# RWKV chunk part: 16 chunks at a time, odd chunks crossing to the other head's partitions, transition matrices per chunk, gate pieces inside the state chain

## What is computed

```python
def step(s, inp):
    r_t, w_t, k_t, v_t, a_t, b_t = inp
    sa = jnp.einsum('nhvk,nhk->nhv', s, a_t)
    s = (s * w_t[:, :, None, :] + sa[..., None] * b_t[:, :, None, :]
         + v_t[..., None] * k_t[:, :, None, :])
    return s, jnp.einsum('nhvk,nhk->nhv', s, r_t)
```

## Time and profile before

| | us |
|---|---|
| median of 3 runs | 2684.76 (2681.96 to 2686.89) |
| profiled execution | 2676.91 |
| its span, first to last instruction | 2675.2 |
| TensorE busy in it | 2428.9 |

### The profile page before, as it was taken

How to read it: one execution, slowest core, us unless ns; L and a number is a source line. 1 busy time by engine, 2 the same in 40 slices (tenths; PEclk the granted TensorE clock), 3 DMA queues, 4 the chain that set the end, 5 groups by cost and what they waited for, 6 DMA issues and landing times.

```text
span 2675.2 us, 39291 instructions
## 1 busy us (share of the span) xinstructions
PE 2428.9 (91%) x17425; PEld 1629.9 (61%) x17425; DVE 925.3 (35%) x1626; ACT 457.0 (17%) x946; POOL 158.9 (6%) x269
## 2 busy tenths in 40 slices
PE   5998999898888898888879997999999999999994
PEld 3665665557656766756756664666666666666563
DVE  3962441035325415415514333333331013333222
ACT  4114121122113113113130001111110001111002
POOL 2700000000000000000100000000000000000001
PEclk8999999999998998998979998999999999999997
DMA  6101233410020020011033311111101011110101
GB/s 220 60 20 41 78 120 111 132 56 16 11 58 15 8 61 15 8 38 46 3 137 106 128 32 32 32 33 33 33 29 44 24 64 33 33 33 25 36 20 65
DMA packets 111367, 139.72 MB, mean 52 GB/s; under 512 B 14818, under 2 KB 85975, under 8 KB 111184
## 3 DMA queue, kind: packets, MB, share of 16 engines
q1 hardware_dynamic: 96512, 115.38, 13.3%
q10 hardware_dynamic: 10992, 15.21, 1.6%
q0 software_dynamic: 3696, 6.64, 0.9%
HBM read 117.59 MB, written 19.61 MB: 51 GB/s over the span
## 4 chain that ended last, share of the span: by engine, by line
PE 79%; DVE 11%; ACT 4%; DMA 3%; issue 2%; DVEq 0%; ACTq 0%; SPq 0%; POOL 0%; POOLq 0%
PE ps L623 77%; DVE arena L1669 5%; DVE arena L1672 2%; DMA W<-in_w_in_dram 2%; PE ps L627 1%; DMA arena<-in_x_prompt_dram 1%; ACT Y L1437 1%; DVE arena L2100 1%; ACT arena L1316 0%; DMA Y<-in_x_prompt_dram 0%; DVE hT L1672 0%; DVE hT L1669 0%; DVE arena L2037 0%; ACT arena L1362 0%; DVE s5v L1669 0%
## 5 line engine op out<-in xcount | busy, mean ns | idle before, releaser
L623 PE MATMUL ps<-hT,W 128*128 128x352 f32 x4368 | 1337.1, 467 | 53.7 <-DMA W<-in_w_in_dram 17.8
L623 PEld LDWEIGHTS ps<-hT,W 128*128 128x128 f32 x4368 | 837.0, 193 | 528.8 <-issue 58.3
L623 PE MATMUL ps<-arena,W 128*128 128x352 f32 x1440 | 432.0, 463 | 14.7 <-DVE arena L1669 11.9
L623 PE MATMUL ps<-arena 64*64 64x64 f32 (+6 forms) x8744 | 354.6, 232 | 55.2 <-DVE arena L1669 22.0
L623 PEld LDWEIGHTS ps<-arena,W 128*128 128x128 f32 x1440 | 276.1, 192 | 170.1 <-DVE arena L1669 12.5
L623 PEld LDWEIGHTS ps<-arena 64*64 64x64 f32 (+3 forms) x8744 | 300.7, 137 | 115.7 <-issue 43.0
L1316 ACT ACTIVATE arena<-ps 128x512 f32<-128x512 f32 (+7 forms) x235 | 113.2, 489 | 523.1 <-PE ps L623 318.9
L2214 DVE TENSOR_SCALAR Y<-Y,PAR 128x1024 f32<-128x1024 f32 x88 | 49.0, 557 | 426.4 <-ACT Y L1316 424.7
L1316 ACT ACTIVATE Y<-ps 128x352 f32<-128x352 f32 (+3 forms) x220 | 69.9, 350 | 715.2 <-PE ps L623 536.5
L1669 DVE TENSOR_TENSOR arena<-arena 128x1056 f32<-128x1056 f32 (+6 forms) x181 | 166.8, 922 | 59.8 <-PE ps L623 44.9
L1669 DVE TENSOR_TENSOR arena<-ps,arena 128x256 f32<-128x256 f32 (+3 forms) x188 | 99.0, 527 | 220.4 <-PE ps L623 164.0
(11 more groups left out here) (250 smaller groups left out, 995.7 us busy)
## 6 DMA issues: line engine op xcount, KB each, us to landing
W<-in_w_ada_dram SPq DMA_DIRECT2D x12, 2048.0 KB, 9.4
W<-in_w_up_dram SPq DMA_DIRECT2D x22, 1024.0 KB, 6.5
gates<-arena ACTq DMA_DIRECT2D x72, 176.0 KB, 1.8
arena<-gates SPq DMA_DIRECT2D x24, 528.0 KB, 3.5
...
```

What stands on the lines that cost most here:

```text
L623: return nc.tensor.matmul(out, lhsT, rhs, start=start, stop=stop, skip_group_check=True)
```

## The change

The 16 chunks of a pair are taken together. In most products odd chunks cross: one side of the product (source or target) is the head's own half `hp`, the other is `sd` = `side(c, hh)`, and even and odd chunks write different banks. Two groups stay on the own half: `zt`, and the turned A. The halves of a level are now the first and the last 8 chunks. X starts as copies of the unit matrix (ACT) into which DVE copies the product of A and B by a mask, and XT is X turned by TensorE. LT has its own place for all 16 chunks.

The chain changes its form. Before it, and for all chunks, TensorE makes U0 (the part of U that doesn't depend on the state), a transition matrix `Gm` per chunk (unit matrix added by DVE), the state's change without the old state (accumulated in banks 4 and 5 and left open), a corrected R, and the output without the old state (left open in banks 0 and 1). A chain step is then one product of `Gm` with the state on top of the open bank and one scaling by DVE (`carry`), which writes the next state `Sb`; the product of the state with the corrected R finishes the output. After each of the 15 steps one product of gate group 5 or 6 is issued. The sample group's steps have gate group 7 in pieces of 2 products and the first half of group 8 between them; the final prompt state is turned at the end of the pair. The diff, with indentation and many lines left out:

```diff
-Vt, Bt, Kt_ = (carve(16164 + 512 * i, 8, RCH) for i in range(3))
-LA = carve(17700, 8, 2, RCH)
-KA = carve(18724, 8, 2, RCH)
-X, XT, Yb, LTm = (carve(19748 + 512 * i, 8, RCH) for i in range(4))
+LA, KA = carve(11940, 16, 2, RCH), carve(13988, 16, 2, RCH)
+X, XT = carve(16164, 16, RCH), carve(17188, 16, RCH)
+VB, Kt_ = carve(18212, 2, 2, 2, 4, RCH), carve(20260, 16, RCH)
+Yb, LT = carve(1065, 16, RCH), carve(3195, 16, RCH)
+LTm, Gm, Sb = carve(7332, 16, RCH), carve(8868, 16, RCH), carve(10404, 16, RCH)
+W0, U0, YT = X, Yb, LT
+dX, dXT, dLT, dYb, dLTm = (carve(8420 + 64 * i, RCH) for i in range(5))
...
-LT = [C1[:, 512 * i:512 * i + 512].rearrange("p (c t) -> p c t", c=8) for i in range(2)]
...
+def lane(c):
+return 8 * (c // 8) + 4 * (c % 2) + c % 8 // 2
+def vb(c, kind):
+return VB[:, c // 8, c % 2, kind, c % 8 // 2, :]
...
-    for bt in range(2):
-        pool.wait_ge(sem("la_ev"), 5 * (2 * j + bt) + 2)
-        for l in range(1, 6):
-            n = lt_count(j, bt, l)
-            if n > 2:
-                pool.wait_ge(sem("yy_done"), 2 * (n - 2))
-            pool.tensor_tensor(LT[n % 2], LA[:, :, 0, :],
+    for l in range(1, LEVELS):
+        for s in range(2):
+            if l == 1:
+                pool.wait_ge(sem("la_ev"), 5 * j + s + 2)
+            else:
+                pool.wait_ge(sem("yy_done"), level_at(j, l - 1, s))
+            pool.tensor_tensor(LT[:, 8 * s:8 * s + 8, :], LA[:, 8 * s:8 * s + 8, 0, :],
...
+    def both(bt):
+        for c in range(8 * bt, 8 * bt + 8):
+            for hh in range(2):
+                yield c, c % 2, c % 8 // 2, half_of(hh), side(c, hh)
...
-        for x, (b, src) in enumerate(((0, Vp), (1, Bp), (2, Kp))):
-            take(b)
-            for c in range(8):
-                m = heads(lambda hp: mm(pb[b][hp, 64 * c:64 * c + 64], src[hp, 8 * bt + c, :], idS[hp, :]))
-            m.then_inc(sem("tk_done"), 1)
-            give("tk_ev", b)
...
+        for c, par_, i, hp, sd in both(bt):
+            m = mm(pb[par_][sd, col64(c // 2)], ARp[hp, c, 0, :], Bp[hp, c, :])
+    m.then_inc(sem("la_done"), 1)
+    give("la_ev", 0, 1)
+    def with_a_r(src, bt):
+        b = 4 + 2 * bt
+        take(b, b + 1)
+        for c, par_, i, hp, sd in both(bt):
+            m = mm(pb[b + par_][sd, P * i:P * (i + 1)], src[hp, c, :],
+                   ARp[hp, c, :, :].rearrange("p a b -> p (a b)"))
         m.then_inc(sem("la_done"), 1)
...
+    with_a_r(Bp, 0)
+    with_a_r(Bp, 1)
+    take(2, 3)
+    for bt in range(2):
+        for c, par_, i, hp, sd in both(bt):
+            m = mm(pb[2 + par_][sd, col64(c // 2)], Kp[hp, c, :], idS[hp, :])
+    m.then_inc(sem("tk_done"), 1)
+    give("tk_ev", 2, 3)
+    values_b(0)
+    with_a_r(Kp, 0)
+    with_a_r(Kp, 1)
+    values_b(1)
+    pe.wait_ge(sem("la_ev"), 5 * j + 1)
+    for bt in range(2):
+        take(2 * bt, 2 * bt + 1)
+        for c, par_, i, hp, sd in both(bt):
+            m = mm(pb[2 * bt + par_][hp, col64(i)], X[sd, pos(c), :], idS[sd, :])
+        m.then_inc(sem("tk_done"), 1)
+        give("tk_ev", 2 * bt, 2 * bt + 1)
+    take(4, 5)
+    for bt in range(2):
+        for c, par_, i, hp, sd in both(bt):
+            m = mm(pb[4 + bt][hp, col64(4 * par_ + i)], ARp[hp, c, 0, :], idS[hp, :])
+    m.then_inc(sem("tk_done"), 1)
+    give("tk_ev", 4, 5)
...
+    def yy(l, s):
+        pe.wait_ge(sem("lt_ready"), level_at(j, l, s))
+        if l > 1:
+            pe.wait_ge(sem("zx_ev"), 8 * j + 2 * (l - 2) + s + 1)
+        take(2 * s, 2 * s + 1)
+        for c, par_, i, hp, sd in both(s):
+            m = mm(pb[2 * s + par_][hp, col64(i)], LT[sd, lane(c), :], X[sd, pos(c), :])
+        m.then_inc(sem("yy_done"), 1)
+        give("yy_ev", 2 * s, 2 * s + 1)
+    def zt_ready(l, s):
+        pe.wait_ge(sem("yy_ev"), level_at(j, l, s))
+        if l == 1:
+            pe.wait_ge(sem("tk_ev"), 6 * j + 4 + s)
+        else:
+            pe.wait_ge(sem("zt_ev"), level_at(j, l - 1, s))
+    def zx(l, s):
+        zt_ready(l, s)
+        take(2 * s, 2 * s + 1)
+        for c, par_, i, hp, sd in both(s):
+            m = mm(pb[2 * s + par_][sd, col64(4 + i)], XT[hp, lane(c), :], Yb[hp, lane(c), :])
+        m.then_inc(sem("zx_done"), 1)
+        give("zx_ev", 2 * s, 2 * s + 1)
+    def zt(l, s):
+        zt_ready(l, s)
+        take(4 + s)
+        for c, par_, i, hp, sd in both(s):
+            m = mm(pb[4 + s][hp, col64(4 * par_ + i)], Yb[hp, lane(c), :], XT[hp, lane(c), :])
+        m.then_inc(sem("zt_done"), 1)
+        give("zt_ev", 4 + s)
+    last = LEVELS - 1
+    yy(1, 0)
+    yy(1, 1)
+    for l in range(1, last):
+        for s in range(2):
+            zx(l, s)
+            zt(l, s)
+            yy(l + 1, s)
+    pe.wait_ge(sem("la_ev"), 5 * (j + 1))
+    pe.wait_ge(sem("tk_ev"), 6 * j + 3)
+    take(6, 7)
+    for s in range(2):
+        for c, par_, i, hp, sd in both(s):
+            m = mm(pb[6 + par_][hp, col64(c // 2)], KA[sd, lane(c), 0, :], vb(c, 0)[sd, :])
+    m.then_inc(sem("wy_done"), 1)
+    give("wy_ev", 6, 7)
+    for s in range(2):
+        zt(last, s)
+    pe.wait_ge(sem("tk_ev"), 6 * (j + 1))
+    for s in range(2):
+        pe.wait_ge(sem("zt_ev"), level_at(j, last, s))
+        if s == 0:
+            take(0, 1)
+        for c, par_, i, hp, sd in both(s):
+            m = mm(pb[par_][sd, col64(c // 2)], XT[hp, lane(c), :], LTm[hp, lane(c), :])
+        if s:
+            m.then_inc(sem("wy_done"), 1)
+            give("wy_ev", 0, 1)
+        else:
+            take(2, 3)
+            pe.wait_ge(sem("wy_ev"), 2 * j + 1)
+        for c, par_, i, hp, sd in both(s):
+            m = mm(pb[2 + par_][sd, col64(c // 2)], XT[hp, lane(c), :], W0[hp, pos(c), :])
+    m.then_inc(sem("u0_done"), 1)
+    give("u0_ev", 2, 3)
+    take(4, 5)
+    for s in range(2):
+        for c, par_, i, hp, sd in both(s):
+            mm(pb[4 + par_][hp, col64(c // 2)], Kt_[sd, pos(c), :], vb(c, 0)[sd, :], c < 2, False)
+    pe.wait_ge(sem("wy_ev"), 2 * (j + 1))
+    take(6, 7)
+    for s in range(2):
+        for c, par_, i, hp, sd in both(s):
+            m = mm(pb[6 + par_][hp, col64(c // 2)], YT[sd, pos(c), :], vb(c, 1)[sd, :])
+    m.then_inc(sem("gm_done"), 1)
+    give("gm_ev", 6, 7)
+    pe.wait_ge(sem("u0_ev"), j + 1)
+    for s in range(2):
+        for c, par_, i, hp, sd in both(s):
+            m = mm(pb[4 + par_][hp, col64(c // 2)], vb(c, 1)[sd, :], U0[sd, pos(c), :], False, False)
+    m.then_inc(sem("gm_done"), 1)
...
+    take(2, 3)
+    for s in range(2):
+        for c, par_, i, hp, sd in both(s):
+            m = mm(pb[2 + par_][hp, col64(c // 2)], YT[sd, pos(c), :], LA[sd, lane(c), 1, :])
+    m.then_inc(sem("gm_done"), 1)
+    give("gm_ev", 2, 3)
+    take(0, 1)
+    for s in range(2):
+        for c, par_, i, hp, sd in both(s):
+            mm(pb[par_][hp, col64(c // 2)], vb(c, 0)[sd, :], KA[sd, lane(c), 1, :], c < 2, False)
+            m = mm(pb[par_][hp, col64(c // 2)], U0[sd, pos(c), :], LA[sd, lane(c), 1, :], False, False)
+    m.then_inc(sem("y_part"), 1)
+    for c in range(1, 16):
+        par_, i = c % 2, c // 2
+        pe.wait_ge(sem("s_ready"), 16 * j + c)
+        if c == 1:
+            pe.wait_ge(sem("gm_ev"), 2 * j + 1)
+        heads(lambda hp: mm(pb[4 + par_][hp, col64(i)], Gm[hp, pos(c), :], Sb[hp, c - 1, :], False, True))\
+            .then_inc(sem("ds_done"), 1)
+        if c == 1:
+            pe.wait_ge(sem("y_part"), j + 1)
+            pe.wait_ge(sem("gm_ev"), 2 * j + 2)
+        m = heads(lambda hp: mm(pb[par_][hp, col64(i)], Sb[hp, c - 1, :], ARp[hp, c, 1, :], False, True))
+        gates_part(8 + j, 5 + (c - 1) // 8, (c - 1) % 8, (c - 1) % 8 + 1)
+    m.then_inc(sem("ry_done"), 1)
+    give("ry_ev", 0, 1)
...
+    gates_part(8 + j, 6, 7, KT)
...
         m = heads(lambda hp: mm(gt4[hp, :, ts_], Sin[hp, n, :], ARp[hp, 16, :, ts_]))
     m.then_inc(sem("dec_done"), 1)
     give("dec_made", 4)
-    gates_part(8 + j, 5, 0, KT, 2)
+    gates_part(8 + j, 7, 0, 2)
     pe.wait_ge(sem("dec_made"), 4 * j + 1)
-    take(1)
-    heads(lambda hp: mm(pb[1][hp, 0:64], LT[0][hp, 0, :], X[hp, 0, :])).then_inc(sem("dec_done"), 1)
-    give("dec_copied", 1)
+    take(5)
+    heads(lambda hp: mm(pb[5][hp, 0:64], dLT[hp, :], dX[hp, :])).then_inc(sem("dec_done"), 1)
+    give("dec_copied", 5)
+    gates_part(8 + j, 7, 2, 4)
     pe.wait_ge(sem("dec_made"), 4 * j + 2)
...
+    give("dec_made", 3)
+    gates_part(8 + j, 7, 4, 6)
...
-    gates_part(8 + j, 6, KT // 2, KT)
+    gates_part(8 + j, 7, 6, KT)
...
-    gates_part(8 + j, 7, 0, KT, 3)
-    pe.wait_ge(sem("ry_ev"), 3 * (j + 1))
+    give("ry_ev", 2)
+    gates_part(8 + j, 8, 0, 4)
...
+        m = heads(lambda hp: mm(pb[7][hp, 64 * n:64 * n + 64], Sout[hp, n, :], idS[hp, :]))
     m.then_inc(sem("so_done"), 1)
-    give("rw_rows", 6)
-    heads(lambda hp: mm(pb[7][hp, 0:64], S2[hp, 0, :], idS[hp, :])).then_inc(sem("so_done"), 1)
     give("rw_rows", 7)
-    gates_part(8 + j, 8, 0, KT, 4)
+    gates_part(8 + j, 8, 4, KT)
...
```

(81 more changed lines are left out.)

250 lines of the change are left out of this document (62 added, 188 removed).

## The result

The changed kernel takes 2619.44 us (median of 4, 2614.35 to 2623.78) against 2683.38: ratio 0.976, 95% interval 0.974 to 0.978. It is faster by 2.4 to 2.7%, and less than half of the 142 us forecast; 2619 lies above the range, whose end was 2590. The profiled execution took 2614.35. All times are medians over the executions of a kernel; of e11's six, two, of 4790 and 8065 us, are left out (in the second, whose trace is kept, a full-width product instruction took 1334 ns in the mean for 469).

What follows compares the result with a forecast made beforehand. TensorE's busy time and idle spots were taken as the bound. A pair falls from 115.6 to 80.1 us (39.0 dense, 17.5 chain, 23.6 behind); 142 us off 2676.91 gives 2535, or 2543 on the median's scale; range 2520 to 2590.

Steps and rivals of the forecast that it cites:

- the first four items of "The new chunk part": Pair's work ahead of the chain: first products and transposes, first level, eight half levels, products behind them; 39.0 us.
- Crossing at 15 ns: Crossing products in the chunk part: 15 ns per 64-column instruction, against 29.6 in the diagonal order.
- The feeding rival: Purely crossing stretches: code blocks at 2.6 us each hold TensorE up, +22 us, 2565; chance 0.13.
- the two on ACT: TensorE's waits for ACT before the levels: 0.8 for the last V and B, about 1.0 for the turned A.
- The tie in the levels: Half levels: the diagonal group's 0.96 covers the add; costed at nothing, without cover up to 0.95 x 8.
- The chain: 15 state steps of 1.17 us each, gate piece and switching included, above the 0.76 round trip; 17.5 us a pair.
- Behind it: The pair's part after the chain: 33.5 us falls to 23.6, mainly by 8.9 of gates moved away.
- The gap at the pair's end: TensorE's wait for DVE that begins the next pair: some 6.7 us, unchanged.
- Sum: A whole pair: 115.6 us before, 56.5 + 23.6 = 80.1 after; 35.5 x 4 = 142 us saved.
- crossing does nothing here: Chunk part: crossing gains no pace, 62 us for the 39, pair 103, total 2635; chance 0.04.
- The clock rival: The whole new chunk part runs at 1.2 GHz: the pair takes 131, total 2748, slower; chance 0.02.

Runs made afterwards that it cites:

- e11: e6 with two chunks turned by one product, gate group 5 moved into the first three levels, group 6 at every other chain step; 2591.13, ratio 0.965.
- e1: The changed kernel with every product kept on its head's own half, so no crossing; 2639.43, ratio 0.985.
- e7: The changed kernel with gate group 5 moved from the chain into the first three levels and group 6 behind the levels; 2619.35, ratio 0.977.
- e10: The changed kernel with gate groups 5 and 6 whole behind the chain and none in it; 2638.93, ratio 0.984.
- e12: e6 with gate group 5 moved into the first three levels and group 6 in the chain at every other step; 2599.68, ratio 0.970.
- e2: The changed kernel with the corrected R's crossing products issued four times, 192 more crossing instructions a pair; 2631.33, ratio 0.982.
- e3: The changed kernel with the last level's own-half group issued four times, 192 more own-half instructions a pair; 2632.40, ratio 0.982.
- e4: The changed kernel with four more full-width products a pair in the dense stretch behind the levels, results never read; 2615.56, ratio 0.976.
- e6: The changed kernel with products that share a stationary operand merged into one of 128 columns, 128 product instructions less a pair; 2594.81, ratio 0.968.

## Why the prediction was wrong

The direction was right and the size was not. The step that failed is the first four items of "The new chunk part": 39.0 us by TensorE's pace, 58.9 measured (58.6 without the chain's first 8 instructions, which that window holds). The chain and what stands behind it came out.

- *Crossing at 15 ns:* right inside a block (127 in 2.0 us), wrong as an average. The HGRN2 rows that it rested on have 64 to 68 instructions between gates: too short a burst to ask for code faster than it comes. Over the dense part an instruction takes 30 ns, the own-half pace. That pace was itself read from a burst of 96: the earlier trace rows also have 480 own-half instructions in 15.82 us, 33 ns each, and e1 has 31.6.
- *The feeding rival* named the mechanism and the place, but took 2.6 us a block and half the blocks, +22 us. It is 3.8 us (the four windows' mean of 59.6 over 15.6 blocks), and holds in the levels too, where 128 instructions need 2.6 to 2.8 by themselves. It stood as a gap "between 1.1 and 3.8 that no row fills"; the kernel before ran at 3.8 us a block without a stall, so it had shown only an upper bound. Taking that bound (15.5 blocks x 3.8 = 59 us) would have given the measured 58.9, by luck in part: nothing in the trace before says that the supply lies just at the bound. It got 0.13, too little for a gap that no row filled. (The Trainium skill, Runtime: NRT & Kernel Launch, Instruction fetch mechanics, calls the refill mostly hidden. These runs disagree for products of 15 ns: 12.4 us of "issue" in 58.9.)
- *Waits:* the two on ACT came (0.75 and 0.87 for 0.8 and 1.0). The tie in the levels held: no wait for DVE's adds in the first pair, one of 0.2 in the last. A half level still takes 2.24 for 1.92 (642.74 to 644.98), of which 0.16 is a wait for POOL's mask, which the prediction put at nothing. One wait was missed, 0.42 at 625 for DVE's copy of the bonus sums, which holds bank 4. In the first pair the granted clock, 0.58 from 635 to 639, costs some 1.4 more (94 instructions from 635.07 in 3.7 us; e7's take 2.3).
- *The chain:* 1.17 a step forecast and measured, TensorE never idle. That switching between 64x64 and full-width work costs 0.34 a round trip fits it.
- *Behind it:* 23.6 forecast, 23.4 measured (from 699.36 to 722.76). The gap at the pair's end, 6.7, is 6.45.
- *Sum:* 58.6 + 17.5 + 23.4 = 99.5 for 80.1, so 19.4 x 4 = 78 us by the first pair; the profiled execution, 2614.35, is 79 above the 2535. The four dense parts together are 3 us longer than four times the first.
- *Other rivals:* crossing does nothing here gave 2635, and e1, which has no crossing, measured 2639, so the rest of the sum holds at the own-half pace. As an account of the changed kernel it was wrong: 127 crossing instructions pass in 2.0 us, and crossing is worth 1.0 to 1.2% of the kernel. The clock rival, a stretch of 64x64 work at 1.2 GHz, costs 1.4 us in the changed kernel's first pair and some 1.5 at the start of the third chain (two steps in the 3.86 from 1065.41 to 1069.27, for 2.34), but weighs more in the chains of e7 and e10, which have no gates, and in some of e12's.
- *What is shown:* that the stalls go with the count of instructions in the stream follows from e2 against e3, from e4 and from e6. That it is the fetch of code, and nothing else that goes with the count, rests on the packets' distance and was not separated further.
